# Modulation chunks in four column groups, other places for them, and squares added ahead of their sums

## The reference, cut to what matters

```python
mod_l = jnp.split(sc @ w_mod[i] + b_mod[i], 6, axis=-1)     # sc = silu(c), w_mod[i]: 1024 x 6144
mod_c = jnp.split(scc @ w_mod[i] + b_mod[i], 6, axis=-1)
hl = modulate(rms_norm(xl, norm1_g[i]), mod_l[0], mod_l[1])
ol = conv_module(hl, ...)        # layer 0: h @ w_pw1, gate, 31 taps along the tokens, layer_norm, silu, @ w_pw2
xl = xl + mod_l[2][:, None, :] * ol
hl = modulate(rms_norm(xl, norm2_g[i]), mod_l[3], mod_l[4])   # then the MLP
```

## Time and profile before

| | us |
|---|---|
| median of 3 runs | 2456.91 |
| lowest, highest | 2452.63, 2457.16 |
| profiled execution | 2456.01 |
| its span, first to last instruction | 2454.4 |
| PE busy | 2278.9 (93%) |
| DVE busy | 1388.2 (57%) |
| ACT busy | 780.7 (32%) |
| POOL busy | 679.7 (28%) |
| chain that ended last: PE, DVE | 84%, 7% |

### The profile page before, as it was taken

One profiled execution on the slowest core, in us unless ns is written; L12 is line 12 of the kernel. 1 busy time (PEld: TensorE's weight loads), 2 busy tenths in 40 slices (PEclk: granted clock), 3 DMA queues, 4 the chain that ended last, 5 costly groups with the idle time before them and its releaser, 6 DMA issues.

```text
span 2454.4 us, 30001 instructions
## 1 busy us (share of the span) xinstructions
PE 2278.9 (93%) x11308; PEld 1792.8 (73%) x11308; DVE 1388.2 (57%) x1776; ACT 780.7 (32%) x1064; POOL 679.7 (28%) x363
## 2 busy tenths in 40 slices
PE   7999889999999999897999899999899679799994
PEld 5677548788888888773456788887688567688883
DVE  5799923374444445406662755545222851699995
ACT  3111113311111111332662211112233322577773
POOL 0000002333333333333434344444444034011111
PEclk8999979999999999999999899999999999899997
DMA  8533444172122221120002233333233023499994
GB/s 295 171 103 103 155 129 162 35 267 68 60 68 60 60 69 61 58 86 9 1 1 60 87 95 94 95 96 112 70 94 95 1 72 137 174 390 407 405 408 183
DMA packets 248297, 312.79 MB, mean 127 GB/s; under 512 B 13482, under 2 KB 199563, under 8 KB 235923
## 3 DMA queue, kind: packets, MB, share of 16 engines
q1 hardware_dynamic: 236716, 275.33, 33.1%
q0 software_dynamic: 6688, 25.69, 2.7%
q10 hardware_dynamic: 4807, 10.58, 1.1%
HBM read 286.39 MB, written 25.18 MB: 127 GB/s over the span
## 4 chain that ended last, share of the span: by engine, by line
PE 84%; DVE 7%; issue 4%; POOL 2%; ACT 2%; DMA 2%; DVEq 0%; POOLq 0%; SPq 0%; ACTq 0%
PE acc L507 52%; PE acc L2519 7%; PE pb L2537 4%; PE acc L541 2%; PE acc L2279 2%; PE pb L2130 2%; PE pa L2293 2%; PE pb L2306 2%; PE pb L2074 1%; PE pa L2074 1%; PE acc L571 1%; POOL wlo L497 1%; PE acc L585 1%; DVE hid_hi L1537 1%; PE pa L2509 1%
## 5 line engine op out<-in xcount | busy, mean ns | idle before, releaser
L497 POOL TENSOR_TENSOR wlo<-raw,whi 128x1024 fp32r<-128x1024 f32 x204 | 507.7, 2489 | 1054.5 <-ACT whi L486 1054.4
L486 ACT ACTIVATE whi<-raw 128x1024 fp32r<-128x1024 f32 x218 | 230.1, 1059 | 1038.0 <-PE acc L507 977.8
L507 PE MATMUL acc<-ah,whi 128*128 128x512 f32 (+1 forms) x1448 | 458.2, 363 | 18.1 <-POOL wlo L497 9.8
L507 PE MATMUL acc<-ah,wlo 128*128 128x512 f32 (+1 forms) x1448 | 454.0, 360 | 0.0
L507 PE MATMUL acc<-al,whi 128*128 128x512 f32 (+1 forms) x1448 | 452.9, 360 | 0.0
L507 PEld LDWEIGHTS acc<-ah,whi 128*128 128x128 f32 x1448 | 272.3, 189 | 67.1 <-POOL wlo L497 12.1
L507 PEld LDWEIGHTS acc<-al,whi 128*128 128x128 f32 x1448 | 273.4, 189 | 42.2 <-issue 0.5
L507 PEld LDWEIGHTS acc<-ah,wlo 128*128 128x128 f32 x1448 | 273.1, 189 | 42.0
L1546 DVE SCALAR_TENSOR_TENSOR x<-acc,mod,x 128x256 f32<-128x256 f32 (+1 forms) x192 | 121.1, 658 | 262.0 <-PE acc L507 262.0
L778 DVE TENSOR_TENSOR expert_lo<-expert_pair,expert_hi 128x1024 fp32r<-128x1024 f32 x192 | 225.0, 1219 | 15.5 <-ACT expert_hi L773 15.4
L507 PE MATMUL acc<-hid_hi,whi 128*128 128x512 f32 (+1 forms) x768 | 230.7, 355 | 0.7 <-DVE x L1546 0.2
(11 more groups left out here) (368 smaller groups left out, 3032.1 us busy)
## 6 DMA issues: line engine op xcount, KB each, us to landing
raw<-in_w_ff SPq DMA_DIRECT2D x128, 512.0 KB, 3.9
mod_raw<-in_w_mod SPq DMA_DIRECT2D x76, 512.0 KB, 5.3
expert_pair<-in_expert_w_gate SPq DMA_DIRECT2D x32, 1024.0 KB, 8.0
expert_pair<-in_expert_w_up SPq DMA_DIRECT2D x32, 1024.0 KB, 7.8
expert_pair<-in_expert_w_down SPq DMA_DIRECT2D x32, 1024.0 KB, 7.3
raw<-in_w_in SPq DMA_DIRECT2D x30, 512.0 KB, 3.9
raw<-in_conv_w_pw SPq DMA_DIRECT2D x24, 512.0 KB, 4.8
expert_rows_dram<-zero_rows POOLq DMA_DIRECT2D x1, 12288.0 KB, 38.2
```

What stands on the lines that cost most here:

```text
L486: e.eng.activation(whi[e.n["q"] % 2][:, :], raw[r][:, :], ACT.Copy).then_inc(S["hi_ready"], 1)
L497: e.eng.tensor_tensor(wlo[b][:, :], raw[e.n["g"] % RING][:, :], whi[b][:, :].bitcast(F32), ALU.subtract).then_inc(S["lo_ready"], 1)
L507: ins = e.eng.matmul(o, w, m, start=keys.index(key) == n, stop=len(keys) - 1 - keys[::-1].index(key) == n)
```

## The change

- The ring and the list of tiles: tiles 0 to 6 have two chunks each, tile 7 has chunks 18 to 21, and 22 and 23 stand before and after the next pair of products. The last chunk goes through the ring.
- `mod_piece` uses 32 columns of silu(c) and four groups of 32 PSUM partitions; `mod_pick` adds four groups.
- Chunk 5 is multiplied after the products of tile 1, not before them; the turns of chunks 0 and 1 follow the sums of the first norm, and chunks 2 and 3 both follow the spreading of its root.
- The chunks of tile 7 go to the two halves of `acc[1]`, their columns to `acc[0]`, and don't wait for DVE's taking of the taps.
- DVE adds the squares of tiles 4 to 7 to those of tile 3, and PE sums four tiles in place of eight, with no pieces of chunks between.
- Chunks no longer stand in the second norm.

```diff
--- before.py
+++ after.py
@@ -54,7 +54,7 @@
 PE_TAPS = (0, 6, 6, 6, 6, 6, 6, 9)
-CHUNKS_OF_TILE = ((4, 5), (6, 7), (8,), (9,), (10,), (11,), (12,), (13, 14, 15, 16, 17))
+CHUNKS_OF_TILE = ((4, 5), (6, 7), (8, 9), (10, 11), (12, 13), (14, 15), (16, 17), (18, 19, 20, 21))
 LAST_CHUNKS = CHUNKS_OF_TILE[-1]
@@ -232,7 +232,6 @@
-    mod_last = sb("mod_last", [P, KT, 512], at=h_at)
     mod_early = [sb(f"mod_early{n}", [P, KT, 512], at=ah_at + 16384 * n) for n in range(2)]
@@ -450,7 +449,7 @@
-    ring_chunks = [n for n in range(23) if early_place(n) is None]
+    ring_chunks = [n for n in range(24) if early_place(n) is None]
@@ -577,15 +576,15 @@
-    def sum_over_channels(e, src, ready, done0, beside):
-
-        for t in range(KT):
-            e.eng.wait_ge(S[ready], done0 + t + 1)
+    def sum_over_channels(e, src):
+
+        for t in range(4):
+            e.eng.wait_ge(S["ln_sq_ready"], t + 1)
+            if t == 3:
+                e.eng.wait_ge(S["ln_added"], KT - 4)
             for b in range(TOK // P):
                 ins = e.eng.matmul(acc[0][:, 0:6], src[:, t, b * P:b * P + P], to_token_column(b),
-                                   start=t == 0 and b == 0, stop=t == KT - 1 and b == 5)
-            if t < KT - 1:
-                beside(t)
+                                   start=t == 0 and b == 0, stop=t == 3 and b == 5)
         ins.then_inc(S["stat_ready"], 1)
@@ -612,7 +611,7 @@
         at = 512 + 8 * (n - LAST_CHUNKS[0])
-        return pbk[:, at:at + 8 * count]
+        return (acc[0] if n in LAST_CHUNKS else pbk)[:, at:at + 8 * count]
@@ -817,16 +816,11 @@
                     load_pw(5 + 2 * i)
-        for n in (18, 19, 20):
-            mod_load(e, n)
+        mod_load(e, 22)
         load_pw(20)
         load_pw(21)
-        sp.wait_ge(S["stat_ready"], 3)
-        sp.dma_start(mod_last[:, :, :], A["w_mod"][1, :, 11 * 512:12 * 512].rearrange("(k p) n -> p k n", p=P)
-                     ).then_inc(S["mod_last_in"], 16)
-        mod_load(e, 21)
+        mod_load(e, 23)
         load_pw(22)
-        mod_load(e, 22)
         load_pw(23)
@@ -1001,15 +995,16 @@
                 split_first(e, split_high)
+                if i == 1:
+                    copy_row(5, pa[:, 0:512])
                 copy_row(chunks[0], pa[:, 0:512])
...
                 make_diagonals(i + 1)
-                for n in chunks[1:]:
-                    copy_row(n, pa[:, 0:512])
+                if i:
+                    copy_row(chunks[1], pa[:, 0:512])
             else:
-                copy_row(chunks[0], pa[:, 0:512])
-                for n in chunks[1:]:
-                    copy_row(n, pbk[:, 0:512])
+                for n in chunks:
+                    copy_row(n, acc[1][:, 512 * (n % 2):512 * (n % 2) + 512])
         e.n["u"] += 2 * KT
@@ -1023,8 +1018,6 @@
                            ).then_inc(S["ln_sq_ready"], 1)
-        copy_row(18, pbk[:, 0:512])
-        copy_row(19, acc[1][:, 0:512])
         early()
@@ -1034,20 +1027,13 @@
             act.activation(ah[:, i, :], y[:, i, :], ACT.Copy).then_inc(S["ah_ready"], 1)
-        copy_row(20, pbk[:, 0:512])
-
+        copy_row(22, pbk[:, 0:512])
         split_first(e, high)
-        copy_row(21, pa[:, 0:512])
+        copy_row(23, pa[:, 0:512])
         for _ in range(KT - 3):
...
         e.n["u"] += KT
-        rows_left = [22, 23]
-
-        def early_and_row():
-            copy_row(rows_left.pop(0), pbk[:, 0:512])
-            early()
-
-        norm_act(e, 1, 2, FULL, 3, early_and_row, AFFINE[1])
+        norm_act(e, 1, 2, FULL, 3, early, AFFINE[1])
@@ -1392,7 +1378,8 @@
         dve.wait_ge(S["mats_in"], 16)
-        TT(mod_pick[:, :], mats[:, M_ID, 0:2], mats[:, M_ID, HD:HD + 2], ALU.add).then_inc(S["prepared"], 1)
+        dve.tensor_reduce(mod_pick[:, :], mats[:, M_ID, :].rearrange("p (g c) -> p c g", g=4)[:, 0:2, :], AX.X, ALU.add
+                          ).then_inc(S["prepared"], 1)
@@ -1500,6 +1487,10 @@
                ).then_inc(S["centred"], 1)
+        for t in range(4, KT):
+            dve.wait_ge(S["ln_sq_ready"], t + 1)
+            TT(sq[:, 3, :], sq[:, 3, :], sq[:, t, :], ALU.add).then_inc(S["ln_added"], 1)
+            dve.wait_ge(S["ln_added"], t - 3)
         inverse_root(e, 3, FULL, 2, sums=acc[0])
@@ -1512,10 +1503,10 @@
                 ln_scale(i + 3)
-        modulation(18, 2, late_rows(18, 2))
-        dve.wait_ge(S["mod_added"], 20)
+        dve.wait_ge(S["mod_added"], 22)
         scales(1, 0, 4, V_N2)
-        e.step(scales(2, 1, 1, V_N1B))
+        scales(2, 1, 1, V_N1B)
+        e.step(scales(3, 1, 4, V_N2B))
@@ -1551,9 +1542,7 @@
         norm_dve(e, 1, 4, FULL, 3, 2, AFFINE[1])
-        modulation(20, 4, late_rows(20, 4))
-        dve.wait_ge(S["mod_added"], 24)
-        scales(3, 1, 4, V_N2B)
+        modulation(22, 2, late_rows(22, 2))
@@ -2062,16 +2051,12 @@
                 pe.wait_ge(S[f"mod_early_in{early[0]}"], early[1])
-            elif n < 23:
+            else:
                 pe.wait_ge(S[f"mod_in{r}"], 16 * ring_chunks.index(n) + 16)
-            else:
-                pe.wait_ge(S["mod_last_in"], 16)
             for k in range(2):
-                if early:
-                    rows = mod_early[early[0]][:, 2 * r + k, :]
-                else:
-                    rows = mod_raw[r][:, k, :] if n < 23 else mod_last[:, 2 * r + k, :]
-                ins = pe.matmul(bank[HD * k:HD * k + HD, :], silu_c[:, 2 * r + k, :], rows, start=r == 0, stop=r == 3)
+                rows = mod_early[early[0]][:, 2 * r + k, :] if early else mod_raw[r][:, k, :]
+                part = 32 * ((2 * r + k) % 4)
+                ins = pe.matmul(bank[part:part + 32, :], silu_c[:, 2 * r + k, 0:32], rows, start=r < 2, stop=r >= 2)
                 if after_product and r == 0 and k == 0:
@@ -2093,10 +2078,14 @@
             mod_chunk(n, acc[0][:, 512 * n:512 * n + 512])
-        for n in range(2):
-            turn_mod(n, pbk[:, 8 * n:8 * n + 8])
-        spread_mean(e, 0, FULL, 1, lambda: mod_chunk(2, acc[1][:, 0:512]))
-        mod_chunk(3, acc[1][:, 512:1024])
+
+        def turn_scales():
+            for n in range(2):
+                turn_mod(n, pbk[:, 8 * n:8 * n + 8])
+
+        spread_mean(e, 0, FULL, 1, turn_scales)
+        for n in (2, 3):
+            mod_chunk(n, acc[1][:, 512 * (n - 2):512 * (n - 2) + 512])
         for n in (2, 3):
@@ -2132,30 +2121,31 @@
         pair(FULL, 0)
-        for i in range(KT - 1):
-            chunks = CHUNKS_OF_TILE[i]
-            mod_chunk(chunks[0], pa[:, 0:512], after_product=True)
-            if i:
-                conv_taps(i)
-            pe.wait_ge(S["mod_added"], chunks[0])
-            turn_mod(chunks[0], turned_at(i, chunks[0]))
-            if len(chunks) > 1:
-                mod_chunk(chunks[1], pa[:, 0:512])
+        mod_chunk(4, pa[:, 0:512], after_product=True)
+        project(2)
+        pe.wait_ge(S["mod_added"], 4)
+        turn_mod(4, turned_at(0, 4))
+        project(3)
+        mod_chunk(5, pa[:, 0:512], after_product=True)
+        turn_mod(5, turned_at(0, 5))
+        for i in range(1, KT - 1):
+            first, second = CHUNKS_OF_TILE[i]
+            mod_chunk(first, pa[:, 0:512], after_product=i > 1)
+            conv_taps(i)
+            pe.wait_ge(S["mod_added"], first)
+            turn_mod(first, turned_at(i, first))
+            mod_chunk(second, pa[:, 0:512])
             project(2 * i + 2)
-            if len(chunks) > 1:
-                turn_mod(chunks[1], turned_at(i, chunks[1]))
+            turn_mod(second, turned_at(i, second))
             project(2 * i + 3)
         conv_taps(KT - 1)
-        def turned_late(n):
-            return late_rows(n, 1)
-
-        mod_chunk(LAST_CHUNKS[0], pa[:, 0:512], after_product=True)
-        pe.wait_ge(S["conv_taken"], KT - 1)
-        pe.wait_ge(S["mod_added"], LAST_CHUNKS[0])
+        pe.wait_ge(S["acc_free"], e.at("u", 2))
         for n in LAST_CHUNKS:
-            turn_mod(n, turned_late(n))
-            if n < LAST_CHUNKS[-1]:
-                mod_chunk(n + 1, pbk[:, 0:512])
+            if n >= LAST_CHUNKS[2]:
+                turn_mod(n - 2, late_rows(n - 2, 1))
+            mod_chunk(n, acc[1][:, 512 * (n % 2):512 * (n % 2) + 512], after_product=n == LAST_CHUNKS[0])
+        for n in LAST_CHUNKS[-2:]:
+            turn_mod(n, late_rows(n, 1))
         pe.wait_ge(S["late_in"], 96)
@@ -2164,35 +2154,23 @@
         ins.then_inc(S["stat_ready"], 1)
-        beside_sums = {0: [(18, 0)], 1: [(18, 1)], 2: [(18, 2)], 3: [(18, 3), (19, 0)], 4: [(19, 1)], 5: [(19, 2)],
-                       6: [(19, 3)]}
-
-        def pieces_beside(t):
-            for n, r in beside_sums.get(t, []):
-                mod_piece(n, r, (pbk if n == 18 else acc[1])[:, 0:512])
-            if t == 6:
-                pe.wait_ge(S["mod_added"], 18)
-                turn_mod(18, turned_late(18))
-
-        sum_over_channels(e, sq, "ln_sq_ready", 0, pieces_beside)
-        turn_mod(19, turned_late(19))
+        sum_over_channels(e, sq)
```

(18 more changed lines are left out.)

## The result

The changed kernel took 2424.1 us (median of 4 runs, 2415.4 to 2433.3) against 2454.8 for the kernel before on the same chip: ratio 0.987 (0.985 to 0.990). Two more comparisons of the same two kernels gave 2417.3 against 2456.6, ratio 0.985 (0.982 to 0.987), and 2423.1 against 2457.0, ratio 0.986 (0.982 to 0.989). The change saves 31 to 39 us, where 49.5 were forecast. All three medians lie in the stated range of 2398 to 2434, and all three above the forecast's own range of 2399 to 2414.

A forecast was written before the change was run, and what follows sets the result against it. PE and DVE nearly full in the convolution loop; most to win after it, where DVE waits 32.8 us for PE's sums. Terms -4.0 - 3.0 + 5.3 - 11.4 - 25.7 - 10.7 = -49.5: median 2407, range 2398 to 2434, own range 2399 to 2414.

The forecast's parts named there:

- A: Start, up to the first pair of products: sums first, chunks 2 and 3 beside y; -4.0 us, bounds -2 and -6.
- the price of chunk 23: After the next pair of products: chunk 23 stands in place of chunk 21, with four groups; -1.7 us.
- F: After the next pair: chunk 23 for 21, -1.7, and y of the next norm 6.7 after the last product, -9.0; -10.7 us.
- rival 1: Modulation chunks: only two groups run at a time, a chunk stays at 3.58; +26, 2433 us; chance 0.15.
- rival 2: A wait for ACT's copy or chunk weights returns in each tile, half clock holds through first pair; 2416 us; chance 0.11.
- Price of a chunk: Modulation chunk of 8 matmuls: four column groups side by side take 1.86 us, where two groups took 3.58.
- Rivals 1 and 3: Besides rival 1: four groups run one after another, 7.1 us a chunk, +95, 2502 us; chance 0.04.
- B: Tiles 0 and 1: -7.7 and +4.7, together -3.0 us; chunk 5 and the DMA wait move into tile 1.
- C: Tiles 2 to 6: two chunks each, 30.6 us a tile for 29.53, +1.07 in five tiles; +5.3 us.
- D: Tile 7 up to the first subtraction: four chunks directly behind the taps, DVE's convolution decides; -11.4 us, bounds -13 and 0.
- E: Layer norm: 13.9 us from first subtraction to statistics for 39.8, four adds at 4.2; with spreading and pair, -25.7 us.
- After it: Stages behind those changed, such as the MLP: only shifted in time, 0 us.

The follow-up runs named there:

- the experiment on the order of the start: Changed kernel with the first norm's old order: turns of chunks 0 and 1 ahead of the sums, chunk 2 ahead of the spreading; 2415.4 us (one run).
- fillers: Changed kernel plus matmuls whose result nobody uses, where PE would idle ahead of half-clock stages at the start and in the layer norm; 2421.1 us, ratio 0.986.

## Why the prediction was right in kind and too large

The mechanism of most steps was right, and no rival took its place; two steps failed (A, and the price of chunk 23 within F), and other terms of the sum were mis-sized, nearly all on the side of too much gain. That the time fell into 2398 to 2434 is owed in part to luck: that range reached so far because of rival 1, a chunk of 3.58, and rival 2, waits in each tile, and neither came; the forecast's own range was missed by 3 to 10 us. In the order of the prediction's steps:

- **Price of a chunk**: 1.85 for 1.86. Rivals 1 and 3 are out by the loads and by the experiment with two groups. The estimate of 2.2 from the Trainium skill (TensorE: Matmul & The Clock Gate, "Part 3: Packing small matmuls") is too high here, and its rule that loads overlap running matmuls only when the row group differs does not hold for four column groups on all rows either: the loads of 0.13 lie inside chunks that take no longer for them.
- **A, start, -4.0: failed.** The means give -0.2, and from DVE's last add of squares the gain is 0.1 to 2.0 (see the experiment on the order of the start). The prediction took sums of 1.53 and turns of 1.9 at full clock; they took 2.73, 2.56 and 3.42, and the spreading 2.93 for 1.5. The price of a sum was taken from the second norm, while the chain of the kernel before had these very sums slower:

```profile
29.67 2.02 PE pa L661 x12
31.69 2.56 PE pa L666 x12
```

  With two short chunks PE is done early and idles 2.5 to 3.8 until the squares are added, and most of what stands behind runs at a granted clock of 0.50. The bound of -2 "if the half clock lasts" named the true case, which rival 2 had counted too, but allowed too little for it; of rival 2's other waits, in each tile, none came. With fillers the pair starts at 46.3, 1.3 later than forecast.
- **B, -3.0**: right, -2.4. Tile 0 took 21.2, tile 1 38.8, with a DMA wait of 4.90.
- **C, +5.3**: +6.1. A tile takes 30.6 to 30.9.
- **D, -11.4**: -10.5. The last mean product took 2.94, for 2.6, at half clock; DVE's convolution decides, as said.
- **E, -25.7**: -25.4 in the pair of profiles that the prediction was made from, but the second profile of the kernel before has this stage 3.2 shorter (two of its eight sums took 1.66 and 1.54, not 2.66), so -23.8 in the means. Within it the adds were mis-sized: 5.95 for 4.2. Three take 0.97 and the last 2.99 in all three profiles of the changed kernel. The chain in the third and the last add:

```profile
335.26 0.97 DVE sq L1492
336.25 2.99 DVE sq L1492
```

  The timeline of POOL beside it:

```profile
335.36 3.05 POOL L496 TENSOR_TENSOR wlo<-raw,whi 128x1024 fp32r<-128x1024 f32 x1 [34.47 <-ACT whi L485]
```

  In the run without adds the same low part stands at the same place (after 34.47 of idle, as here) and is shorter:

```profile
334.43 2.35 POOL L496 TENSOR_TENSOR wlo<-raw,whi 128x1024 fp32r<-128x1024 f32 x1 [34.47 <-ACT whi L485]
```

  So the adds are what makes POOL's record 0.70 longer. The times fit engines that take turns: the third add runs its usual 0.97 and ends 0.87 after POOL's record begins, and the last add ends 0.8 after POOL's (338.41), nearly its usual length. That POOL is what makes the last add long is argued from these times; no run took the low part away.
- **F, -10.7**: -8.2, or -7.4 in the means. Two parts failed. The low part after the first product (L496, POOL) was the wait behind chunk 23, so a shorter chunk wins nothing there (with two groups the chunk takes 3.58 and PE goes on without that wait):

```profile
367.07 2.38 POOL wlo L496
369.49 17.23 PE acc L506 x96
```

  From 365.87 to 369.49 PE waits 3.6, just the 3.58 that chunk 21 had taken: the -1.7 had been counted without asking what ends next. And y of the second norm comes 8.7 after the last product (422.41), not 6.7: in the profile shown the sums run at half clock, 2.66 for 1.53, and the spreading as well (in the second profile the sum takes 1.78).

```profile
424.75 2.66 PE pa L665 x12
```

- **After it, 0**: the forecast took for granted that what is only shifted keeps its length. The MLP can change by 10 us from one execution to the next, more than all terms but three.

By the means the shortfall is 15.8: start 3.8, loop 1.4, tile 7 0.9, layer norm 1.9, after the pair 3.3, MLP and rest 4.1, first pair 0.3 (they sum to within rounding). The half clock is the largest single cause that is under a kernel's hand, by the first profile's rows: sums, turns and spreading at the start (5 us, of which the fillers won back 2), spreading and sums in the second norm (about 2) and the last sums of the layer norm (1.3).

## What to carry to other kernels

Where work is taken off an engine, ask what clock it then has: behind a wait that the change opens, a stage of PE can cost nearly double (here 2.73 for 1.50), so price it by the row of that very place, at both clocks. A shortened step is worth nothing where another wait ends at the same time; look for the second latest releaser (here POOL's low part behind chunk 23) before taking its price. When starts vary from run to run, reckon a stage from the event that releases it, and take the last such event, not the last one on the chain. Compare stages over two or more profiles of each kernel, as a single pair can hide 10 us in a part that the change doesn't touch.

## What the runs showed of the hardware

- Four column groups run side by side as two do: 8 matmuls of 512 columns in 1.85 us for 3.58, against an estimate of 7.1 one after another, by the price of the taps.
- The stream of the MLP's matmuls at a granted clock of 1.00 has two paces, 8.32 and 8.48 us for 48 of them, in both kernels. Thirteen profiles keep one of them through the MLP of layer 0; in the one with small breaks in the stream it changed at one of eight breaks.
- An fp32 addition of DVE of 128x768 took 0.97 three times and 2.99 once, the latter beside a subtraction of POOL of 128x1024, which itself took 3.05 there and 2.34 to 2.38 elsewhere, 2.35 at the same place when DVE added nothing.
- The 12 records of a sum took 2.73, 2.73 and 1.83 after PE had idled 3.75, 2.54 and 3.04, 1.50 after it had idled 2.37, and 1.40 right behind the fillers: the idle time just before them does not tell which clock they get.
